# Leaving out the products without a reader at eight borders of a two-block transformer kernel

## What is computed

```python
for l in range(DEPTH):                      # first block
    x = x + 0.5 * mx[:, 2] * swiglu(ada_norm(x, norm_g[l, 0], mx[:, 0], mx[:, 1]), ffn_w_in[l, 0], ffn_w_out[l, 0])
    hx = ada_norm(x, norm_g[l, 1], mx[:, 3], mx[:, 4])
    yx, yc = even_mixer(...) if l % 2 == 0 else odd_mixer(...)
    x = x + mx[:, 5] * yx
    x = x + 0.5 * mx[:, 8] * swiglu(ada_norm(x, norm_g[l, 2], mx[:, 6], mx[:, 7]), ffn_w_in[l, 1], ffn_w_out[l, 1])
# second block, per layer
    x = _layer_norm(alpha * x + g1 * y, ln1_g[i], ln1_b[i])
    x = _layer_norm(alpha * x + g2 * _mlp(x * (1 + sc2) + sh2, mlp_w1[i], mlp_w2[i]), ln2_g[i], ln2_b[i])
```

## The kernel before

| place | code | products |
|---|---|---|
| program's begin | L958 | 4 |
| norm n01, into the even mixer | `warm_sum`, table `WARM` | 5 |
| norm n02, into ffn01 | same | 9 |
| norm n10, into ffn10 | same | 5 |
| norm n11, into the odd mixer | same | 5 |
| first piece of the odd mixer's second output half | `kept_warm`, L1033 | 8 |
| layer norm ln10, ahead of its sums | L685 | 6 |
| first piece of mlp1 | `kept_warm`, L1022 | 9 |
| layer norm ln11, the program's last | L685 | 6 |

## Time and profile before

### The profile page before, as it was taken

One profiled execution on the slowest core, in us unless ns is written; L12 is line 12 of the kernel. 1 busy time (PEld: TensorE's weight loads), 2 busy tenths in 40 slices (PEclk: granted clock), 3 DMA queues, 4 the chain that ended last, 5 costly groups with the idle time before them and its releaser, 6 DMA issues.

```text
span 2931.3 us, 44027 instructions
## 1 busy us (share of the span) xinstructions
PE 2828.8 (97%) x17694; PEld 2492.6 (85%) x17694; DVE 2013.9 (69%) x3397; ACT 1281.7 (44%) x2121; POOL 339.3 (12%) x380
## 2 busy tenths in 40 slices
PE   7999999998999999999999989999999999999998
PEld 6888898666888889888897889999979999887898
DVE  7789956555687656788655775666656689767764
ACT  4222244354422224222245565565455554645653
POOL 0000011322100001000011110022102210300100
PEclk8999999899999999999999999999999999999999
DMA  6666522011455534556432234455425579653453
GB/s 245 222 223 230 201 85 94 29 51 43 145 201 208 212 125 158 201 205 210 145 113 80 72 130 151 149 176 174 164 81 172 187 277 327 199 155 101 137 187 115
DMA packets 141194, 467.63 MB, mean 160 GB/s; under 512 B 27024, under 2 KB 29200, under 8 KB 140480
## 3 DMA queue, kind: packets, MB, share of 16 engines
q1 hardware_dynamic: 125440, 408.20, 41.2%
q0 software_dynamic: 15552, 56.63, 5.5%
HBM read 463.73 MB, written 1.05 MB: 159 GB/s over the span
## 4 chain that ended last, share of the span: by engine, by line
PE 80%; DVE 11%; ACT 5%; issue 2%; DMA 2%; POOL 1%; SPq 0%; ACTq 0%; DVEq 0%; POOLq 0%
PE bank L2657 24%; PE bank L2658 24%; PE bank L2659 24%; DVE sb_split_low L2061 3%; DVE sb_h_low L2148 1%; DMA sb_raw<-weights 1%; PE bank L2929 1%; PE bank L3100 1%; PE bank L2948 1%; DMA sb_ada_mlp<-ada 1%; DVE sb_temp L2075 1%; PE bank L2889 1%; DVE sb_x_res L2264 1%; DVE sb_temp L2142 1%; ACT sb_temp L1966 1%
## 5 line engine op out<-in xcount | busy, mean ns | idle before, releaser
L2657 PE MATMUL bank<-sb_h_high,sb_split_high 128*128 128x256 f32 (+1 forms) x3464 | 1116.6, 322 | 39.5 <-DVE sb_h_low L2156 16.5
L2658 PE MATMUL bank<-sb_h_low,sb_split_high 128*128 128x256 f32 (+1 forms) x3464 | 1097.8, 317 | 0.0
L2659 PE MATMUL bank<-sb_h_high,sb_split_low 128*128 128x256 f32 (+1 forms) x3464 | 1097.1, 317 | 0.0
L1646 ACT ACTIVATE sb_split_high<-sb_raw 128x1024 fp32r<-128x1024 f32 x620 | 646.4, 1051 | 306.6 <-PE bank L2659 286.2
L2061 DVE TENSOR_TENSOR sb_split_low<-sb_raw,sb_split_high 128x1024 fp32r<-128x1024 f32 x620 | 758.6, 1232 | 21.6 <-ACT sb_split_high L1646 21.5
L2657 PEld LDWEIGHTS bank<-sb_h_high,sb_split_high 128*128 128x128 f32 x3464 | 666.7, 192 | 100.9 <-issue 17.7
L2658 PEld LDWEIGHTS bank<-sb_h_low,sb_split_high 128*128 128x128 f32 x3464 | 667.8, 193 | 40.8
L2659 PEld LDWEIGHTS bank<-sb_h_high,sb_split_low 128*128 128x128 f32 x3464 | 667.0, 193 | 40.7
L2075 DVE CUSTOM_DVE_ANT_0 sb_temp<-sb_ada_ffn,sb_cond_ffn 128x1024 bf16<-128x1024 f32 x364 | 429.7, 1220 | 25.1 <-DMA sb_ada_ffn<-ada 16.0
L2657 PE MATMUL bank<-sb_hidden_high_ffn,sb_split_high 128*128 128x512 f32 (+1 forms) x830 | 280.4, 338 | 0.0
L2659 PE MATMUL bank<-sb_hidden_high_ffn,sb_split_low 128*128 128x512 f32 (+1 forms) x830 | 279.2, 336 | 0.0
(11 more groups left out here) (329 smaller groups left out, 3498.2 us busy)
## 6 DMA issues: line engine op xcount, KB each, us to landing
sb_raw<-weights SPq DMA_DIRECT2D x620, 512.0 KB, 3.4
sb_ada_ffn<-ada SPq DMA_DIRECT2D x114, 512.0 KB, 4.6
sb_ada_ffn<-ada POOLq DMA_DIRECT2D x90, 512.0 KB, 3.8
sb_ada_mlp<-ada POOLq DMA_DIRECT2D x18, 512.0 KB, 5.6
sb_ada_mlp<-ada SPq DMA_DIRECT2D x18, 512.0 KB, 5.9
sb_cond_ffn<-cond SPq DMA_DIRECT2D x3, 1024.0 KB, 5.4
sb_na_raw<-na_rpb SPq DMA_DIRECT2D x32, 96.0 KB, 6.8
sb_x_res<-tokens SPq DMA_DIRECT2D x4, 512.0 KB, 7.7
```

Source lines behind the costliest of these rows:

```text
L1646: do.activation(m.high[s % HIGHS][:, :], m.raw[s % RAWS][:, :], identity).then_inc(*act.mark("split_high", s))
L2657: do.matmul(out, ah, bh, start=start and j == 0, stop=False)
L2658: do.matmul(out, ah, bl, start=False, stop=False)
L2659: last = do.matmul(out, al, bh, start=False, stop=stop and j == len(terms) - 1)
```

## The change

`warm` returns at once unless it is asked for exactly four products. The one call with four is that at the program's begin; the eight calls with 5, 9, 5, 5, 8, 6, 9 and 6 emit nothing, neither products nor their waits.

```diff
     def warm(bank, n):
 
+        if n != 4:
+            return
         pe.wait_ge("inputs", "all")
         free(bank)
         for _ in range(n):
```

## The result

The changed kernel is slower, by 0.28%: a median of 2943.46 us over 17 runs against 2934.80 us over 17 runs of the kernel before, ratio 1.0028 with a 95% interval of 1.0018 to 1.0037, that is +5.3 to +10.9 us, with 8.2 us as the likeliest (the two medians by themselves lie 8.7 us apart). The forecast for the median was 2939.2 us; the measured one is in the stated range (2932.5 to 2945.5), but more than 0.2% above the kernel before, where the forecast had only 0.33 of its chances.

The account below looks back on a forecast made before the run. TensorE's stream of products, busy 97%, was taken as the bound. Terms 2.3 + 1.5 + 0.7 + 0.5 + 0.5 - 0.7 = +4.8 us on a median of 2934.4 gave 2939.2 us, range 2932.5 to 2945.5.

Parts of the forecast that it names:

- No time gained where the sum waits anyway: At seven of eight places the next real instruction waits for POOL or VectorE, so removing products gains nothing there.
- Rival 4: The products were on the path, so up to 22.8 us come back: 2911.6 us; chance 0.05.
- rival 3: Mixers and VectorE's chains absorb all lateness, only ln11 is left: -0.7, so 2933.7 us; chance 0.05.
- ln11, -0.7 us: At the program's end, sums no longer run behind the products; L2733 starts at 2919.45 instead of 2920.16, gaining 0.7 us.
- n01, n10, n11: 3 x 0.75 = 2.3 us: At three norms with 2.4 us waits, half a chance each of a half-clock stretch; bounds 0 and 1.5 each.
- Rival 2: The three waits of 2.4 us keep the clock, only long ones lose it: +2.5, so 2936.9 us; chance 0.20.
- The price of one stretch, 1.5 us: Where TensorE is full, a half-clock stretch misses 14 records, 1.6 us, taken as 1.5.
- n02: 1.5 us: At norm n02, idle 5.3 us, one half-clock stretch nearly surely: 1.5 us, bounds 1.4 and 3.0.
- Odd output: 0.7 us: Odd mixer's second output half: a stretch nearly surely, partly absorbed by the VectorE-held stage behind; 0.7, between 0 and 1.5.
- ln10 and mlp1: 1.0 us together: ln10's narrow sums at half clock, 0.5 (0 to 1); mlp1's existing stretch earlier or longer, 0.5 (0 to 1.5).
- Rival 1, the half clock lasts for two stretches: Two stretches (3.0 us) at n01, n02, n10 and n11, the first not filled: +13.0, so 2947.4 us; chance 0.25.
- The rule of the Trainium skill: TensorE's default state is throttled and activity releases it, so the removed products were holding the clock: slower, not -22.8 us.

Follow-up runs that it names:

- e1_norms_off: Kernel before without the 24 products at the four norms n01, n02, n10 and n11, the other 29 kept; ratio 1.0019 (1.0008 to 1.0030), +5.6 us.
- e3_narrow: Kernel before with all 53 products and their waits kept, each narrowed from 256 columns to 2; ratio 1.0032 (1.0019 to 1.0044).
- e5_short_off: Kernel before without the 15 products at n01, n10 and n11, all others kept; ratio 1.0019 (1.0011 to 1.0028), +5.6 us.
- e8: Kernel before with more products: 12 at n02, 10 at ln10, 17 ahead of mlp1, 5 new in mlp0, none at ln11; ratio 1.0004 (0.9995 to 1.0013).
- e6: Kernel before without the nine products at n02 alone; ratio 0.9998 (0.9989 to 1.0006).
- e12: The kernel of e6 again, without n02's nine products, in a new series against the kernel before; ratio 1.0006 (0.9997 to 1.0015).

## Why the prediction was right in kind and low in size

- *No time gained where the sum waits anyway.* Right at all seven places. POOL and VectorE end the waits after as before, and the 22.8 us of products were not on the path. Rival 4 is out, and at +8.2 us so is rival 3.
- *ln11, -0.7 us.* Right in sign. The seven profiles without wide products there give -0.18, -0.76, -0.18, -0.31, -0.25, -0.53 and -0.76: a mean of -0.42. Where it is small, the sums themselves ran at half clock: in the changed kernel L2731 starts right when VectorE lets it, but the second group lasts 1.01 us and not 0.58:

```profile
2932.79 0.61 PE L2731 MATMUL bank<-sb_const,sb_rstd 128*128 128x1 f32 x4 [1.50 <-DVE sb_rstd L2192]
...
2933.30 1.01 PE L2735 MATMUL bank<-sb_const,sb_temp 128*128 128x1 f32 x4
```

- *n01, n10, n11: 3 x 0.75 = 2.3 us.* This is the step that failed. I put it that "waits of about 2 to 2.5 us cost the clock about every second time", from single waits of that length elsewhere in the trace. In the changed kernel, e1_norms_off, e3_narrow and e5_short_off these three borders lost the clock 11 times in 12, and n11 had two stretches on end in three of four. The means are 1.1, 1.5 and 2.6 us, in sum 5.2 us in place of 2.3; alone they were timed at +5.6 us (e5_short_off, 1.0019). The third, n11, lies beyond its upper bound of 1.5. Two rows of one execution were too few: at the same two places the fourteen profiles, that of the kernel before among them, show the clock fallen 7 times at the wait of 1.99 us (near 2242) and 11 times at that of 2.32 us (near 2498), so that the latter, which I read as a wait that keeps the clock, was one of three exceptions. And even 18 in 28 is not 11 in 12: the rows had like idle times but other work around them. Rival 2, that short waits keep the clock, is turned round: the short ones are what the change costs.
- *The price of one stretch, 1.5 us.* Right at the border: 1.47 to 1.50 us wherever there was one stretch at n01 and n10. What follows was left out of the terms. The row that gave the price, the stretch at 1141.24, stands 14 us behind n10, and it did not come in any of the four profiles that lost the clock at n10; so 1.4 us of n10's 1.5 are won back. Behind n01 another 1.6 us are lost. That the three local costs, 5.2 us in sum, come so near the timed +5.6 us is luck in so far as these two nearly cancel.
- *n02: 1.5 us.* The profiles have 2.5 to 2.7 us, two stretches on end each time, near the upper bound of 3.0. The repeated times don't show it; open, as above.
- *Odd output: 0.7 us.* The four profiles without wide products there have 1.21, 0.59, 0.36 and 0.60, a mean of 0.7; the nine others lie between -1.1 and 0.0. Right, or a little low.
- *ln10 and mlp1: 1.0 us together.* A mean of 0.9 us in the four profiles with both left out or narrowed (0.56, 1.40, 0.58, 1.23), but of 0.5 us in the six with just before's products there, counting the kernel before as 0. About half was the products' doing. That the stretch at mlp1 costs little was seen; that it costs nothing was not.
- *The sum.* 4.8 us forecast, 8.2 measured. The local costs of the profiles add up to 5.2 + 2.6 + 0.7 + 0.9 - 0.4 = 9.0 us, and of what they have over the forecast the three short borders are 2.9 us and n02 1.1. If n02 costs nothing, as the times have it, the short borders are nearly all of the difference, and the sum without n02 is 6.4 us, still within the measured interval.
- *Rival 1, the half clock lasts for two stretches.* It came true in part: at n02 each time, at n11 mostly, never at n01 or n10. The measured time lies between the forecast and this rival's 2947.4, and on its side of the bound. Its reason, that the first stretch is not filled, fits n02 (PE busy 5.75 of 6.80 us in the changed kernel) and not n11 (6.73 of 6.80 us). Why n11 mostly had two stretches is open.
- *The rule of the Trainium skill* ("TensorE: Matmul & The Clock Gate", "What's actually happening"), that activity releases the throttle, decided the sign. e3_narrow is the run that shows it here: 2 columns in place of 256 cost 1.0032. The begin of the program, which the prediction names as agreeing, says less: the granted clock of the kernel before is 1.0 up to 35.3 us, TensorE's first 9.4 us without work included, and 0.5 only from there to 55.8.

## What to carry to other kernels

Before you delete work that nobody reads, look at what its engine would do instead: on TensorE a gap that other engines cause anyway may be cheaper filled than empty, and a fill of 2 columns a product was worth nothing here. See in a profile that the fill ran in the gap: one of e8's did not. Take the chance of losing the clock from the place itself, by a few profiles without the filler (one in four kept the clock at n01), and not from one wait of the same length elsewhere; and compare the start of the same instruction of another engine across kernels, since that shows a loss of 1.5 us in 2900 which a timed run can't place. Follow it past the border, since the loss can be won back or doubled a little later. Where the next work waits tile by tile for other engines, as at mlp1, a lost clock may cost nothing and need no filler.

## What the runs showed of the hardware that was not expected

- With about 1.4 us idle and 1.17 us of products of 2 columns the clock fell at n01, n10 and n11, three of three; with about 1.5 us idle and about 1.0 us of products of 256 columns it held, three of three in one execution and two of three in another.
- Stretches at half clock come and go between profiles in work that no change touches, which is worth -3.7 to +4.1 us here; e6 and e12, two profiles of one kernel, have 2.65 and 0.56 us. The runs scatter as much (2929.57 to 2943.02 us for the kernel before), which is more than the effect of any one border.
- The stretches at half clock at n02 lasted 6.8 us in each of the eight profiles without wide products there, although TensorE was busy for most of them (5.75 of 6.80 us in the changed kernel), and those at n01 and n10 3.4 us.
